# First attention of a two-block network: softmax factors by ScalarE's logarithm and exponential, and a later place for products and splitting

## The reference

```python
def softmax_with_sink(s, sink):
    sk = sink.astype(jnp.float32)[None, :, :, None, None]
    m = jnp.maximum(jnp.max(s, axis=-1, keepdims=True), sk)
    e = jnp.exp(s - m)
    return e / (jnp.sum(e, axis=-1, keepdims=True) + jnp.exp(sk - m))
...
    def attend_block(args):
        q, k, v, blk = args
        ...
        s_lat = jnp.where(ok, s_lat, NEG_INF)
        s_ctx = jnp.einsum('bqhgd,bkhd->bhgqk', q, k_ctx).astype(jnp.float32)
        p = softmax_with_sink(jnp.concatenate([s_lat, s_ctx], axis=-1), sink_g).astype(v.dtype)
        return (jnp.einsum('bhgqk,bkhd->bqhgd', p[..., :n_loc], v)
                + jnp.einsum('bhgqk,bkhd->bqhgd', p[..., n_loc:], v_ctx))
```

## Time and profile before

| | |
|---|---|
| median of 3 runs | 2657.04 us (2656.43 to 2663.07) |
| the profiled execution's own time | 2659.49 us |
| its span | 2656.7 us |
| PE busy | 2461.1 us (93%) |
| DVE busy | 1693.7 us (64%) |
| ACT busy | 1088.6 us (41%) |
| stretch of the first attention | about 205 to 410 us |

### The profile page before, as it was taken

One profiled execution on the slowest core, in us unless ns is written; L12 is line 12 of the kernel. 1 busy time (PEld: TensorE's weight loads), 2 busy tenths in 40 slices (PEclk: granted clock), 3 DMA queues, 4 the chain that ended last, 5 costly groups with the idle time before them and its releaser, 6 DMA issues. The chain is left out here.

```text
span 2656.7 us, 32750 instructions
## 1 busy us (share of the span) xinstructions
PE 2461.1 (93%) x12252; PEld 2036.7 (77%) x12252; DVE 1693.7 (64%) x2746; ACT 1088.6 (41%) x1739; POOL 94.3 (4%) x111
## 2 busy tenths in 40 slices
PE   6968899899999999899998899998989999999999
PEld 5865558699999997687777688886766666777777
DVE  6666778765646466655553634445347997569986
ACT  4424443431313133423333422333446663377764
POOL 0000000000000000000000000000000330020000
PEclk8989999899999999889999999998999999999999
DMA  6220004133323232011111122222121221149995
GB/s 255 84 91 0 1 1 159 51 133 127 127 96 127 103 127 82 22 48 48 40 40 48 63 97 96 101 91 94 64 72 44 72 71 64 49 164 341 338 336 183
DMA packets 78131, 275.62 MB, mean 104 GB/s; under 512 B 8800, under 2 KB 9312, under 8 KB 77856
## 3 DMA queue, kind: packets, MB, share of 16 engines
q1 hardware_dynamic: 74016, 265.74, 28.5%
q10 hardware_dynamic: 3968, 7.88, 0.9%
HBM read 271.49 MB, written 2.10 MB: 103 GB/s over the span
## 5 line engine op out<-in xcount | busy, mean ns | idle before, releaser
L645 PE MATMUL DP<-HH,WL 128*128 128x384 f32 (+2 forms) x1408 | 517.7, 368 | 28.3 <-DVE WL L638 22.5
L646 PE MATMUL DP<-HH,WH 128*128 128x384 f32 (+2 forms) x1408 | 504.6, 358 | 0.0
L647 PE MATMUL DP<-HL,WH 128*128 128x384 f32 (+2 forms) x1408 | 504.5, 358 | 0.0
L638 DVE TENSOR_TENSOR WL<-RAW,WH 128x1024 fp32r<-128x1024 f32 x230 | 280.8, 1223 | 218.7 <-ACT WH L611 212.0
L645 PE MATMUL DP<-A,WL 128*128 128x384 f32 (+2 forms) x1072 | 381.7, 356 | 22.6 <-issue 8.4
L646 PE MATMUL DP<-A,WH 128*128 128x384 f32 (+2 forms) x1072 | 379.1, 354 | 0.0
L647 PE MATMUL DP<-A,WH 128*128 128x384 f32 (+2 forms) x1072 | 378.8, 353 | 0.0
L611 ACT ACTIVATE WH<-RAW 128x1024 fp32r<-128x1024 f32 x230 | 241.2, 1050 | 292.6 <-PE DP L647 205.0
L645 PEld LDWEIGHTS DP<-HH,WL 128*128 128x128 f32 x1408 | 267.5, 190 | 66.8 <-DVE WL L638 31.8
L646 PEld LDWEIGHTS DP<-HH,WH 128*128 128x128 f32 x1408 | 267.6, 190 | 29.2 <-issue 5.2
L647 PEld LDWEIGHTS DP<-HL,WH 128*128 128x128 f32 x1408 | 267.3, 190 | 25.5
(11 more groups left out here) (419 smaller groups left out, 3863.7 us busy)
## 6 DMA issues: line engine op xcount, KB each, us to landing
RAW<-in_stream SPq DMA_DIRECT2D x326, 512.0 KB, 3.3
MRAW<-in_stream SPq DMA_DIRECT2D x168, 512.0 KB, 5.4
MATS<-in_ssm ACTq DMA_DIRECT2D x16, 256.0 KB, 2.6
X<-in_x SPq DMA_DIRECT2D x8, 384.0 KB, 10.0
BW<-in_rel ACTq DMA_DIRECT2D x4, 512.0 KB, 3.5
out<-X SPq DMA_DIRECT2D x8, 256.0 KB, 2.0
COND<-in_cond SPq DMA_DIRECT2D x1, 1024.0 KB, 4.9
CONST<-in_const SPq DMA_DIRECT2D x1, 256.0 KB, 4.9
```

Of the source, the lines that this page charges most:

```text
L638: dve.tensor_tensor(WL[:, w, :], RAW[:, nxt.u % RING, :], WH[:, w, :].bitcast(F32), ALU.subtract).then_inc(raw_done[nxt.u % RING], 1)
L645: pe.matmul(out, al, bh, start=first, stop=False)
L646: pe.matmul(out, ah, bh, start=False, stop=False)
L647: return pe.matmul(out, ah, bl, start=False, stop=last)
```

## The change

The denominators' reciprocal is formed by ACT as exp(-ln(d)), in `denominators(n)`, straight from the output bank into RC, over all 64x512 repeated denominators; DVE's two transposes and its reciprocal, and the tiles RCT and RCS, go. ACT does it for block n-1 in block n behind `queries_high(n+1)`. DVE's products for block n-1 move behind `maxima(n+2)`, and the splitting of an output (`mixed_high`, `mixed_low`) is done a block later than before. The semaphore `denominators` counts two steps for each block.

```diff
+            def denominators(n):
+
+                act.wait_ge(sem("attended"), values_through(n))
+                if n:
+                    act.wait_ge(sem("normalised"), 2 * n)
+                over = RC[0:64, :, :, :].rearrange("p e j n -> p (e j n)")
+                act.activation(over, XP[64:P, 2 + n % 2, :], ACT.Ln).then_inc(sem("denominators"), 1)
+                act.wait_ge(sem("denominators"), 2 * n + 1)
+                act.activation(over, over, ACT.Exp, scale=-1.0).then_inc(sem("denominators"), 1)
+
@@ -1864,7 +1872,11 @@
                     rows_high(n + 1)
                     queries_high(*WORK[n + 1][0:3])
                 if n:
-                    mixed_high(*WORK[n - 1][0:3])
+                    denominators(n - 1)
+                if n >= 2:
+                    mixed_high(*WORK[n - 2][0:3])
+            mixed_high(*WORK[n - 1][0:3])
+            denominators(n)
             mixed_high(n, g, b)
@@ -2537,16 +2549,8 @@
             def normalise(n):
 
-                dve.wait_ge(sem("attended"), values_through(n))
                 bank_of = 2 + n % 2
-                turned = RCT[:, :].rearrange("p (b n) -> p b n", n=32)
-                dve.transpose(RCT[:, :], XP[64:P, bank_of, :]).then_inc(sem("denominators"), 1)
-                dve.wait_ge(sem("denominators"), 3 * n + 1)
-                dve.reciprocal(RCS[:, :], turned[:, :, 0:1].rearrange("p b n -> p (b n)")).then_inc(sem("denominators"), 1)
-                dve.wait_ge(sem("denominators"), 3 * n + 2)
-                dve.transpose(RC[0:64, :, :, :].rearrange("p e j n -> p (e j n)").rearrange("p (b n) -> p b n", n=32),
-                              RCS[:, :].unsqueeze(2).to_broadcast((64, 16, 32))).then_inc(sem("denominators"), 1)
-                dve.wait_ge(sem("denominators"), 3 * n + 3)
+                dve.wait_ge(sem("denominators"), 2 * n + 2)
                 out = XP[0:64, bank_of, :].rearrange("p (e j n) -> p e j n", e=2, j=2)
@@ -2564,14 +2568,15 @@
             for n, g, b, near, keys, first in WORK:
+                if n + 1 < len(WORK):
+                    rows_low(n + 1)
+                if n >= 2:
+                    mixed_low(*WORK[n - 2][0:3])
+                if n + 2 < len(WORK):
+                    maxima(*WORK[n + 2][0:4])
                 if n:
                     normalise(n - 1)
-                if n + 1 < len(WORK):
-                    rows_low(n + 1)
-                if n:
-                    mixed_low(*WORK[n - 1][0:3])
-                if n + 2 < len(WORK):
-                    maxima(*WORK[n + 2][0:4])
+            mixed_low(*WORK[n - 1][0:3])
             normalise(n)
             mixed_low(n, g, b)
```

More of the change, by code:

```diff
@@ L259, in backbone_kernel @@
             RC = sb(s0, "RC", [P, 2, 2, P])
-            RCT = sb(s0, "RCT", [64, 512])
-            RCS = sb(s0, "RCS", [64, 16])
             OU = sb(s0, "OU", [P, 2, 2, P])
```

## The result

The changed kernel takes 2669.14 us (median of 10 runs, 2662.87 to 2674.51) against 2657.67 us for the kernel before in the same comparison (10 runs, 2653.09 to 2663.07): ratio 1.0039, 95% interval 1.0027 to 1.0051. It is slower by 0.39%, some 10 us (the two medians differ by 11.5); 2672.5 us and 0.58% had been forecast.

What follows compares the result with a forecast made beforehand. PE's in-order stream plus late hand-overs bound the attention, the first row maximum being queued behind ACT. Delays of 14.5 us in blocks 2 to 21 plus 1.0 at the end gave 15.5 us: 2672.5 us, 0.58% more; range 2662 to 2680.

Steps and rivals of the forecast that it cites:

- The first maximum is queued behind ACT, and the pair delays it: In each attention block, ACT's logarithm and exponential ahead of mixed_high move the first row maximum 1.27 us later.
- The pair's price, 1.27 us: ACT's logarithm and exponential of 64x512 per block: 0.59 + 0.03 + 0.63 + 0.02 us; bounds 0.88 and 1.43.
- The slack of the third row score: In block 9, PE's third row score has about 0.24 us of slack behind the first maximum; a longer delay reaches PE.
- kinds 1 and 3: Blocks whose number mod 6 is 1 or 3; PE's third row score delayed by 0.63 and 1.03 us per block.
- Kind 5: Blocks whose number mod 6 is 5, such as block 11; first maximum starts at 307.09 against 306.77, 0.32 us later.
- Products behind the maxima cost nothing: DVE's normalise products after the maxima: PICK waits some 0.25 us in block 11, with nothing lost in the end.
- The end, 1.0 us: Blocks 22 and 23 at the attention's end: the last copy starts at 409.42 instead of 408.41.
- The clock: PE with more holes may get the lower clock for a stretch of the attention; some us allowed above the likeliest case.
- the likeliest case: The whole kernel slowed by ACT's added work delaying the maxima: 2664 to 2676 us, 2672.5 us forecast.
- table changes: Rival: ACT reloads its tables twice in each of 22 logarithm-exponential pairs, 56 us more, 2729 us; 3%.
- swallowed by later waits: Rival: later waits of the same blocks take up PE's delays in kinds 0, 1, 3, 4; 2661 to 2665 us; 10%.
- The hidden case: Rival: logarithm and exponential fit ACT's idle time, leaving rows_low's relief of 0.63 us in 7 blocks; 2652.6 us; 7%.

Runs made afterwards that it cites:

- 1: Changed kernel with mixed_high(n-2) put ahead of denominators(n-1) on ACT; 0.9976 of the kernel before, 2651.0 us.
- 2: Changed kernel with DVE's mixed_low(n-2) put behind the maxima and the products, ACT unchanged; 0.998 of the kernel before, 2653.1 us.
- 5: Changed kernel with ACT's logarithm and exponential done twice in each block; 1.0159 of the kernel before, 2698.05 us.
- 7: Changed kernel with logarithm and exponential over 256 instead of 512 columns from block 2 on; 1.0001 of the kernel before.
- the filled kernel: Changed kernel with the PICK product issued four times instead of once in each two-key block; 1.0027 of the kernel before, 2664.01 us.
- 3: Changed kernel with both reorderings, mixed_high ahead on ACT and mixed_low behind on DVE; 0.9978 of the kernel before, 2651.64 us.

## Why the prediction was right, and where its numbers were off

The measured time lies in the range, and the way was the one forecast. By its own steps:

- *The first maximum is queued behind ACT, and the pair delays it.* Right, and shown from three sides: the wait is seen (37.3 us), it goes when either the copy (1) or the maxima (2) is taken out of the queue, and it scales with the pair (5, 7).
- *The pair's price, 1.27 us.* Mis-sized: the maxima moved by 1.03. The durations were close (0.578 and 0.630 for 0.59 and 0.63), but I put nothing for the border ahead of the pair and a gap of 0.02 behind it, where the instructions overlap by 0.1 each. In 22 places the 0.24 us are 5.3 of the 15.5.
- *The slack of the third row score.* Mis-sized in kinds 1 and 3. A score queued behind a busy PE is recorded as starting while the product ahead of it still runs, and lasts longer: 0.74 at 273.66. Block 7 of the timeline after:

```profile
277.00 2.52 DVE L2533 TENSOR_REDUCE TOP<-DP 128x1 f32<-128x640 f32 x3
...
277.88 0.19 PEld L1186 LDWEIGHTS DP<-KDH,A 128*128 128x128 f32 x1 [0.64 <-DVE TOP L2533]
277.88 0.44 PE L1186 MATMUL DP<-KDH,A 128*128 128x384 f32 x1
```

  It waits, and then lasts 0.44: the 0.30 us that it seems to be late are mostly not lost. Against the start of its block (265.17 before, 269.01 after) the recorded start moved by 0.38 and the recorded end by 0.08, and the block grew by 0.08. In seven blocks of these kinds that is 2 us of the sum.
- *Kind 5.* The forecast took a block's start as fixed against the last steps of the maxima. At the start of block 11 they now end 1.39 us behind it (307.40 against 306.01), where it was 1.63 (302.45 against 300.82), and the queries' copy moves up with them, from 3.23 to 2.99 us behind the block's start: -0.16 instead of +0.32. The starts of block 11, first before, then after:

```profile
300.82 0.40 PE L1209 MATMUL XP<-A,KDH 128*128 128x512 f32 x1
```

```profile
306.01 0.40 PE L1207 MATMUL XP<-A,KDH 128*128 128x512 f32 x1
...
307.23 0.17 DVE L2543 TENSOR_TENSOR SINKS<-SINKD,SHIFT 128x16 f32<-128x16 f32 x1
...
309.00 0.86 ACT L1839 ACTIVATE QB<-A 64x256 fp32r<-64x256 f32 x2
```

- *Products behind the maxima cost nothing.* Right: the blocks have the length that the maxima give them, and the order of 1 keeps the products there and is faster than before.
- *The end, 1.0 us.* It was 0.65; the smaller price, which counts twice in it, would have made it 0.52.
- *The clock.* The prediction allowed "some us" for it above the likeliest case and left it out of the sum. It took 4.1 us of the profiled execution, and 1 in two others. That the holes bring it is shown by the filled kernel as far as three profiles of each go; what else decides over a single fall is not.

So the waits were put at 15.5 us and cost 7.1, and a cost left out of the sum put up to 4 us back. The forecast of 0.58% against 0.39% is nearer than its terms were.

Of the rivals, table changes did not come, and the delays were not swallowed by later waits: kinds 0, 2, 3 and 4 carry theirs into every next block. The hidden case is what 1, 2 and 3 make of the kernel: I had put its relief at 0.63 us for each of 7 blocks, 2652.6 us. It was 0.72, and the kernels measure 2651.0, 2653.1 and 2651.6.

What stays open is why one execution meets four falls and another one, while their blocks without a fall are equal to about 0.02 us.

## What to carry to other kernels

Moving work from a busy engine to an idle one is priced by the queue in which it lands, not by the idle share: ask what stands behind it in that queue, and what stands behind the instruction that waits for that. If the handed-over result is not urgent, put the waiting instruction behind the urgent work on its own engine; here one swap of two lines, on either engine, made a loss of 0.4% a gain of 0.2% (on DVE with one wait more). And when each of some twenty repeated blocks gets a hole of a microsecond on PE, look at the granted clock before adding up the holes.

## What the runs showed of the hardware that was not expected

- Holes of 1.2 to 1.4 us among the row scores of a two-key block were followed by the lower clock at that block's end (1 to 4 times among 7 such blocks), with key scores of 0.63 instead of 0.40 us. With three more products of 128x512 in the same block, at no cost in time, no such fall came in three profiles.
- A 64x512 logarithm from PSUM took 0.578 us and began 0.09 us before the copies ahead of it ended; in experiment 5 both logarithms of a block began 0.02 to 0.03 behind the instruction before, and took 0.59. The same waits stand ahead of the first of them in both kernels, so what makes the difference is open.
